# Preparing queries and keys tile by tile inside the q/k/v projection, with the rest of a convolution beside nine head groups

## What is computed

```python
h  = modulate(rms_norm(x), sh1, sc1);  proj = h @ w_in          # q 512 | k 128 | v 128 | glu 1024
q  = rope(rms_norm(q, q_norm_w));      k = rope(rms_norm(k, k_norm_w))   # per head of 64, 8 q heads, 2 k/v heads
k_ctx = rms_norm(...);  v_ctx = ...                              # context keys: normed, not rotated
s  = q @ [k_ctx, k in a window of +-128].T / 8;  p = softmax([sink, s])   # blocks of 128 queries
u  = ga * sigmoid(gb)
u  = depthwise_conv(u, 31 taps);  u = silu(layer_norm(u))        # 512 channels
x  = x + g1 * (concat(p @ v, u) @ w_out)                         # then the gated MLP
```

## Time and profile before

| what | value |
|---|---|
| median of 3 runs | 1344.73 us (1341.78 to 1345.15) |
| the profiled execution | 1338.05 us |
| its span, first to last instruction | 1336.2 us |
| mean granted TensorE clock | 0.964 |
| PE busy | 1227.3 us (92%) |
| PEld busy | 1014.5 us (76%) |
| DVE busy | 706.0 us (53%) |
| ACT busy | 429.0 us (32%) |
| POOL busy | 171.4 us (13%) |

### The profile page before, as it was taken

One profiled execution on the slowest core, in us unless ns is written; L12 is line 12 of the kernel. 1 busy time (PEld: TensorE's weight loads), 2 busy tenths in 40 slices (PEclk: granted clock), 3 DMA queues, 4 the chain that ended last, 5 costly groups with the idle time before them and its releaser, 6 DMA issues. The chain is left out here.

```text
span 1336.2 us, 15995 instructions
## 1 busy us (share of the span) xinstructions
PE 1227.3 (92%) x6181; PEld 1014.5 (76%) x6181; DVE 706.0 (53%) x950; ACT 429.0 (32%) x831; POOL 171.4 (13%) x146
## 2 busy tenths in 40 slices
PE   6899998259999989989999999999999969999997
PEld 1378887148998967878888888888888858887886
DVE  1489999866566553344434343434344344447445
ACT  4542144355665673443222222222222111111110
POOL 2100000359929100000000000000000000004001
PEclk9899999559999989999999999999999989999999
DMA  9222100015512123213111111111111041113112
GB/s 382 67 76 76 55 1 1 1 64 158 160 62 80 48 90 132 79 48 95 48 48 47 47 47 47 47 47 48 52 55 49 1 157 47 47 48 110 47 47 79
DMA packets 77988, 94.79 MB, mean 71 GB/s; under 512 B 5866, under 2 KB 59234, under 8 KB 76916
## 3 DMA queue, kind: packets, MB, share of 16 engines
q1 hardware_dynamic: 75796, 87.65, 20.2%
q10 hardware_dynamic: 1152, 4.19, 0.8%
q0 software_dynamic: 992, 2.29, 0.5%
HBM read 85.74 MB, written 8.39 MB: 70 GB/s over the span
## 5 line engine op out<-in xcount | busy, mean ns | idle before, releaser
L1281 PE MATMUL ps<-hx,uph 128*128 128x512 f32 x672 | 261.4, 389 | 0.0
L1282 PE MATMUL ps<-hx,uph 128*128 128x512 f32 x672 | 261.4, 389 | 0.0
L1285 PE MATMUL ps<-hx,upl 128*128 128x512 f32 x672 | 206.8, 389 | 0.0
L1083 DVE TENSOR_TENSOR upl<-up_raw,uph 128x1024 fp32r<-128x1024 f32 x44 | 53.8, 1226 | 263.9 <-ACT uph L1080 263.9
L1080 ACT ACTIVATE uph<-up_raw 128x1024 fp32r<-128x1024 f32 x44 | 46.6, 1060 | 339.4 <-PE ps L1285 328.5
L1414 PE MATMUL ps<-dnh,ah 128*128 128x512 f32 x352 | 138.0, 392 | 13.2 <-DVE al L1465 13.2
L1285 PEld LDWEIGHTS ps<-hx,upl 128*128 128x128 f32 x672 | 126.1, 188 | 26.2
L1282 PEld LDWEIGHTS ps<-hx,uph 128*128 128x128 f32 x672 | 126.2, 188 | 26.1
L1281 PEld LDWEIGHTS ps<-hx,uph 128*128 128x128 f32 x672 | 126.1, 188 | 26.2
L1415 PE MATMUL ps<-dnl,ah 128*128 128x512 f32 x352 | 137.5, 391 | 0.0
L1416 PE MATMUL ps<-dnh,al 128*128 128x512 f32 x352 | 137.4, 390 | 0.0
(11 more groups left out here) (241 smaller groups left out, 2169.8 us busy)
## 6 DMA issues: line engine op xcount, KB each, us to landing
up_raw<-in_w_up SPq DMA_DIRECT2D x44, 512.0 KB, 3.8
wm<-in_w_mod SPq DMA_DIRECT2D x32, 512.0 KB, 3.8
dn_raw<-in_w_down SPq DMA_DIRECT2D x44, 256.0 KB, 2.6
wm<-in_w_mod SPq DMA_DIRECT2D x8, 1024.0 KB, 20.2
xs<-in_x ACTq DMA_DIRECT2D x8, 512.0 KB, 14.5
gw_raw<-in_w_in SPq DMA_DIRECT2D x8, 512.0 KB, 4.0
wo_raw<-in_w_out SPq DMA_DIRECT2D x8, 512.0 KB, 3.4
xt<-in_x SPq DMA_DIRECT2D x8, 512.0 KB, 5.2
```

The lines of the kernel that those rows point to most:

```text
L1083: dve.tensor_tensor(out=upl[:, g], in0=up_raw[:, g], in1=f(uph[:, g]), op=ALU.subtract).then_inc(up_lo, 1)
L1281: pe.matmul(o, uph[:, g, k, :], hx[:, k, 0, c_], start=(k == 0), stop=False)
L1282: pe.matmul(o, uph[:, g, k, :], hx[:, k, 1, c_], start=False, stop=False)
L1285: last = pe.matmul(o, upl[:, g, k, :], hx[:, k, 0, c_], start=False, stop=(k == KT - 1))
```

## The change

Block 2 is gone and its work is in block 1, in the loop over the ten tiles.

- **PE** uses three pairs of banks in turn (`slot(m)`) instead of four, and banks 6 and 7 for the transposes. While it projects tile m it transposes the items of tile m-2 (`turn`), after the products of k = 2, 4 and 6: one item per context tile, three per latent tile. Six items are left behind the last tile.
- **ACT** squares the whole tile from PSUM in one instruction, copies out v alone, takes the square root, and writes the high parts `kst` and `qst` of the tile; `place` puts the transposes into `hx` (over the tokens already projected) and `kTc`. The placing of tile m-2 stands in front of the squares of tile m.
- **DVE** builds the tables first, then per tile rotates straight from PSUM (`rotated`), sums the squares with one reduction, adds the two parts of the rotation, norms the keys, and writes the low parts. Queries are not normed: their factor is the `scale` of the exponential and of line 992. POOL has no part in it. Per latent tile DVE runs 3 steps of the convolution.
- **Convolution**: of the 117 steps 24 stay beside the projection; 93 go into attention, 11 in each of groups 0 to 7 and 5 in group 8 (three after each of the first three `maxima`, two after the fourth).
- **Layer norm**: LN = 9, so the means are in groups 9 and 10, the variances in 11 and 12, the root in 12, and the reciprocals two each in groups 13 and 14. POOL scales `cacc` behind them.
- **Modulation vectors**: POOL still scales the 32 pieces, but adds them with a DMA of its own queue that accumulates into `sums`; the four vectors are summed in parallel, eight rounds of four.
- `wo_raw` is loaded once the convolution is done; the low parts of the outputs are stored in other places of `hx` (`out_rows`).

The diff, cut:

```diff
...
+        TAP_QKV = (0, 0) + (3,) * TT
+        TAP_GRP = 11
...
+            items = []
+            for m in range(NK):
+                items += [(m, "k")] if m < CT else [(m, "k"), (m, 0), (m, 1)]
...
+
+            def slot(m):
+                return 2 * (m % 3)
...
-                sp.wait_ge(gl_mm, NGL)
-                sp.dma_start(cs[:], rope.rearrange("w (t p) d -> p w t d", p=P)).then_inc(cs_in, 16)
+                sp.wait_ge(gw_lo, NGL)
+                sp.dma_start(tabs[:, 0:2], rope.rearrange("w (t p) d -> p w t d", p=P)).then_inc(cs_in, 16)
...
+                def turn(it):
+                    m, kind = items[it]
+                    if it == 0:
+                        pe.wait_ge(u_done, CTL)
+                    if it >= 2:
+                        pe.wait_ge(qkT_out, it - 1)
+                    if kind == "k":
+                        pe.wait_ge(k_lo, m + 1)
+                        src = [kst[:, m % 2, j // 2, j % 2, :] for j in range(4)]
+                    else:
...
+                        src = [qst[:, m % 2, 4 * kind + j].rearrange("p v d -> p (v d)") for j in range(4)]
+                    for j in range(4):
+                        last = pe.transpose(ps[:, 6 + it % 2, j * P:(j + 1) * P].bitcast(F32R), src[j], identr[:])
+                    last.then_inc(qkT, 1)
+
+                turned = 0
+                for m in range(NK):
+                    b = slot(m)
+                    if m < 3:
+                        pe.wait_ge(u_done, 3 if m < 2 else CTL)
+                    else:
+                        pe.wait_ge(v_out, m - 2)
+                        pe.wait_ge(k_mul, m - 2)
+                        if m - 3 >= CT:
+                            pe.wait_ge(q_mul, m - 2 - CT)
...
+                        if m >= 2 and k in (2, 4, 6) and turned < items_upto[m - 1]:
+                            turn(turned)
+                            turned += 1
                     last.then_inc(qkv_mm, 1)
+                while turned < len(items):
+                    turn(turned)
+                    turned += 1
...
+                def place(it):
+                    m, kind = items[it]
+                    act.wait_ge(qkT, it + 1)
...
+                    if m < CT:
...
+                    else:
+                        act.wait_ge(qkv_mm, m + 1)
+                        c_ = slice((m - CT) * P, (m - CT + 1) * P)
+                        dst = hx[:, 0:4, 1, c_] if kind == "k" else hx[:, 4 * kind:4 * kind + 4, 0, c_]
+                        src = src.rearrange("p (j k) -> p j k", j=4)
+                    act.activation(dst, src, ACT.Copy).then_inc(qkT_out, 1)
+
+                placed = 0
...
+                for m in range(NK):
+                    b = slot(m)
+                    while m >= 2 and placed < items_upto[m - 1]:
+                        place(placed)
+                        placed += 1
+                    h0 = 0 if m >= CT else NH
                     act.wait_ge(qkv_mm, m + 1)
+                    if m:
+                        act.wait_ge(ssq_done, m)
+                    act.activation(sqb[:, h0:, :], ps[:, b:b + 2, :].rearrange("p b n -> p (b n)")[:, h0 * HD:(NH + NG) * HD].rearrange("p (h d) -> p h d", d=HD),
+                                   ACT.Square).then_inc(sqb_done, 1)
+                    act.activation(vraw[:, m], ps[:, b + 1, NG * HD:KVC].rearrange("p (g d) -> p g d", g=NG), ACT.Copy).then_inc(v_out, 1)
+                    act.wait_ge(ssq_done, m + 1)
+                    act.activation(msq[:, m, h0:], msq[:, m, h0:], ACT.Sqrt, bias=eps_c).then_inc(root_done, 1)
+                    act.wait_ge(k_rot, m + 1)
+                    if m >= 2:
+                        act.wait_ge(qkT, items_upto[m - 2] + 1)
+                    for r in range(2):
+                        act.activation(kst[:, m % 2, :, 0, r * HD:(r + 1) * HD], ka[:, m % 2], ACT.Copy).then_inc(k_hi, 1)
                     if m >= CT:
...
-                        last = act.activation(sqj[:, m % 2, h, :], v, ACT.Square, accum_out=msq[:, m, h:h + 1])
...
+                        act.wait_ge(q_rot, m - CT + 1)
+                        if m - CT >= 2:
+                            act.wait_ge(qkT, items_upto[m - 1])
+                        act.activation(qst[:, m % 2, :, 0, :], h3(qa[:, m % 2, :]), ACT.Copy).then_inc(q_hi, 1)
...
-                taps(CTL * NCS)
...
+                def rotated(out_c, out_s, src, tab, t, heads, first_wait, signal):
...
+                        dve.tensor_tensor(out=b4[:, :, :, half, :], in0=a4[:, :, :, 1 - half, :],
+                                          in1=sn4[:, :, half, :].unsqueeze(1).to_broadcast([P, heads, 2, 16]), op=ALU.mult)
+                    dve.tensor_tensor(out=out_c.rearrange("p (h d) -> p h d", h=heads), in0=src.rearrange("p (h d) -> p h d", h=heads),
+                                      in1=tabs[:, tab, t:t + 1, :].to_broadcast([P, heads, HD]), op=ALU.mult).then_inc(signal, 1)
+
+                for m in range(NK):
+                    b, t, h0 = slot(m), m - CT, (0 if m >= CT else NH)
...
+                    dve.wait_ge(tab_done, 11)
+                    dve.wait_ge(v_out, m + 1)
+                    if m >= 2:
+                        dve.wait_ge(k_lo, m - 1)
+                    if m < CT:
+                        dve.tensor_tensor(out=kk, in0=ps[:, b + 1, 0:NG * HD].rearrange("p (g d) -> p g d", g=NG),
+                                          in1=qkw[:, 1:2, :].to_broadcast([P, NG, HD]), op=ALU.mult).then_inc(k_mul, 1)
                     else:
...
+                        rotated(flat(kk), flat(kr), ps[:, b + 1, 0:NG * HD], 0, t, NG, None, k_mul)
+                        if t >= 2:
+                            dve.wait_ge(q_lo, t - 1)
+                        rotated(qa[:, m % 2, :], qb[:, m % 2, :], ps[:, b, :], 2, t, NH, None, q_mul)
+                    dve.wait_ge(sqb_done, m + 1)
+                    dve.reduce_sum(msq[:, m, h0:], sqb[:, h0:, :], axis=AX.X).then_inc(ssq_done, 1)
+                    dve.wait_ge(k_mul, m + 1)
+                    if m >= CT:
+                        dve.tensor_tensor(out=kk, in0=kk, in1=kr, op=ALU.add).then_inc(k_mul2, 1)
+                        dve.wait_ge(q_mul, t + 1)
+                        dve.tensor_tensor(out=qa[:, m % 2, :], in0=qa[:, m % 2, :], in1=qb[:, m % 2, :], op=ALU.add).then_inc(q_rot, 1)
+                        dve.wait_ge(k_mul2, t + 1)
+                    dve.wait_ge(root_done, m + 1)
+                    dve.reciprocal(msq[:, m, h0:], msq[:, m, h0:]).then_inc(rr_done, 1)
+                    dve.wait_ge(rr_done, m + 1)
+                    dve.tensor_tensor(out=kk, in0=kk, in1=msq[:, m, NH:].unsqueeze(2).to_broadcast([P, NG, HD]), op=ALU.mult).then_inc(k_rot, 1)
+                    taps(dve, TAP_QKV[m])
+                    dve.wait_ge(k_hi, 2 * (m + 1))
+                    dve.wait_ge(k_rot, m + 1)
+                    for r in range(2):
+                        ins = dve.tensor_tensor(out=kst[:, m % 2, :, 1, r * HD:(r + 1) * HD], in0=kk, in1=f(kst[:, m % 2, :, 0, r * HD:(r + 1) * HD]),
...
+                    ins.then_inc(k_lo, 1)
+                    if m >= CT:
+                        dve.wait_ge(q_hi, t + 1)
+                        dve.tensor_tensor(out=qst[:, m % 2, :, 1, :], in0=h3(qa[:, m % 2, :]), in1=f(qst[:, m % 2, :, 0, :]),
+                                          op=ALU.subtract).then_inc(q_lo, 1)
...
-                for n in range(NMOD):
-                    if n >= NW:
-                        sp.wait_ge(mod_acc, n - NW + 1)
...
+                for k in range(KT):
+                    for a, sec in enumerate(SECTIONS):
...
+                sp.wait_ge(tap_done, CTL * NCS)
...
-                    pool.tensor_tensor(out=dst[:], in0=dst[:], in1=w, op=ALU.add).then_inc(mod_acc, 1)
+                for k in range(KT):
+                    for a in range(NW):
+                        pool.wait_ge(wm2_in[a], 16 * (k + 1))
+                        pool.tensor_scalar(wm2[:, a, :], wm2[:, a, :], nat[:, k, 0:1], 1.0, ALU.mult, ALU.mult).then_inc(mod_mul, 1)
...
+                        else:
+                            pool.wait_ge(mod_acc[a], 16 * k)
+                        pool.dma_start(sums[:, a, :], wm2[:, a, :], accum_op=ALU.add).then_inc(mod_acc[a], 16)
+                pool.wait_ge(rec5, 4)
+                for ct in range(CTL):
+                    pool.tensor_tensor(out=cacc[:, ct, :], in0=cacc[:, ct, :], in1=rstd[:], op=ALU.mult).then_inc(scaled, 1)
...
+                    pe.wait_ge(o_lo, n - 1)
+                    if n == LN:
+                        pe.wait_ge(tap_done, CTL * NCS)
+                    if n in (LN, LN + 1):
+                        mean_of(lambda ct: cacc[:, ct, :], n - LN, mean_mm)
+                    else:
+                        pe.wait_ge(sq5, CTL * (n - LN - 1))
+                        mean_of(lambda ct: sqc[ct], n - LN - 2, var_mm)
...
+                    elif n in (LN + 4, LN + 5):
```

(22 more changed lines are left out.)

410 lines of the change are left out of this document (138 added, 272 removed).

## The result

The changed kernel takes 1365.24 us (median of 4 runs, 1363.89 to 1373.56), the kernel before 1344.94 us (4 runs, 1341.78 to 1346.96): a ratio of 1.0166, 95% interval 1.0121 to 1.0211. It is slower, by 20 us: inside the range of the forecast and above the likeliest case's own, which ended at 1360. The profiled execution takes 1363.89 us (span 1362.1), where that of before takes 1338.05: +25.8 us from trace to trace, where the sum of the prediction said +3.7.

The account below looks back on a forecast made before the run. It took PE to wait while DVE works before attention, then to be busy for 180 of 187.5 us. Terms -37.5 - 1.3 + 12.5 + 16 + 14 = +3.7 us gave 1348 us against the median, range 1327 to 1372.

Parts of the forecast that it names:

- the likeliest case: Whole kernel: the forecast of 1348 us, chance 0.52, with its own range of 1338 to 1360 us.
- The start: Projection up to attention: attention starts at 252.1 instead of 289.6 us, -37.5 us, bounds -44 to -30.
- Group 0: First attention group: loses the mean, gets its convolution steps, 20.1 for 21.4 us, -1.3 us.
- Part 3: POOL's scaled pieces beside DVE's steps in attention: thirty pieces at 0.53 us stop steps, +16 us, bounds 0 to 36.
- Part 2: Attention groups 1 to 8: convolution steps on DVE are partly hidden, groups of 13.84 us, +12.5 us (10 to 15).
- the second rival: Groups 0 to 8: PE's clock falls in gaps, costing 15 to 30 us, 1368 us; chance 0.13.
- a clock of 1.00 in groups 1 to 8: Sign to look for in attention: PE's granted clock stays at 1.00 throughout groups 1 to 8.
- the bound of 0: Lower bound for POOL's pieces beside DVE's steps: no cost if steps aren't stopped; dropped by the skill's rule.
- Part 4: Attention groups 9 to 15: layer norm, reciprocals and POOL's scaling come in, POOL's additions go, +14 us (9 to 18).
- the third rival: Modulation sums: accumulating DMAs come one after the other, deciding from 7 us each; at 8 us, 1381 us; chance 0.06.
- the fourth rival: Projection tiles: preparation isn't hidden, PE waits in each, 11.5 us a tile, 16 us more, 1364 us; chance 0.06.
- the first, free steps: Attention: POOL's pieces don't stop DVE's convolution steps, 16 us less, 1332 us; chance 0.23.

Follow-up runs that it names:

- the run with the tables first: Against the changed kernel, the 13 DVE steps behind the last GLU column were issued in the second context tile: 1358.40 us.
- both pieces narrow: Against the changed kernel, the layer norm's four reciprocals and POOL's four scalings of the convolution were cut to 8 columns: 1354.87 us.
- the two last kernels: Changed kernel with rearranged steps (seven per latent tile, nine per group), earlier layer norm: 16 pieces held back, 1325.32 us; none held back, 1330.51 us.

## Why the forecast came out as it did

**The start** was right: -35.6 for -37.5 us. The wait was 6.5 us as predicted, latent tiles are 9.52 to 9.56 us apart from the second on (predicted 9.5), and the end took 10.4 us (243.57 to 253.97). The prediction misread by a slice (PE's hole is slices 6 to 8, counted from 0), its 20 items of 0.34 us make 6.8 and not 6.7, and its sum of a group makes 13.87 and not 13.84; none of it matters. The 1.9 us that were missing lie in two places. The first latent tile's products end 8.4 us later than before (177.50 for 169.12), where the wait and three transposed items make 7.5: the clock fell behind the wait, to 0.88 and 0.78 in the two windows of 10 us from 160 on. The prediction priced the wait alone, and the run with the tables first shows that wait and fall together were worth 9.1 us. The seven tiles from there to 243.57 take 66.1 us, where 59.4 plus 17 items of 0.34 make 65.2.

**Group 0** was wrong by 4.1 us: the step that failed took it as a group at PE's low clock with room for its steps, and put no piece beside it (the thirty pieces of Part 3 are all priced in groups 1 to 8). Four pieces are loaded by then and come in a row; without the scaling it takes 21.2 us (predicted 20.1), so the pieces are 3.0 of the 4.1.

**Groups 1 to 8** came out at +29.9 for +28.5, but by two errors that cancel. That the sum was hit is luck. Taken apart by the run without POOL's scaling: without it they take 116.5 us, +19.7 over before, where Part 2 said +12.5; the pieces add 10.2, where Part 3 said 16. Part 2 had the mechanism and the interval of the maxima right to 1%. It had the end of a group too short, because it took it from a group at full clock. That is the second rival in a small size: the clock did fall, to 0.81 on average from 290 to 390 us. It fell in seven stretches and came back each time. But as DVE sets the pace, it cost some 4 to 7 us (two single pairs of traces) and not the 15 to 30 of the rival. The statement "a clock of 1.00 in groups 1 to 8" was wrong, and groups 1 to 7 took 14.4 to 17.2 us, not 14 to 16. Part 3's mechanism is shown: steps take up to 2.44 us beside a scaling and 0.74 beside a DMA issue. This is what the Trainium skill says ("SBUF — State Buffer", "Who interferes with whom"), and the traces agree; the bound of 0 was rightly dropped. The size of Part 3 was too large: of the 27 scalings in groups 1 to 8 only 15 lengthened a step, by 10.6 us in all.

**Groups 9 to 15** is where the sum failed: +26.5 for +14. Two terms of Part 4 were too small. The means: 14.4 us of products, "less what idle time takes, +11". No idle time takes any. Groups 9 to 12 take 59.4 us where four clean groups take 42.6: +16.8, the products in full and 2.4 for the subtractions in two of them. A stretch in which PE is busy for 180 of 187 us could have said so. The last groups: reciprocals +4.6 and POOL's scaling +1.5 make 6.1, and groups 13 to 15 take 12.8 us more than before (36.3 for 23.5). Eleven of these go away with both pieces narrow. The term left out that a stall there can drop the clock for all that follows, as it did in this trace, and it priced the scaling by its end ("2 us before ACT asks for it") and not by the small sums that it stops. This is the very row that carried Part 3. ACT's root was moved as well and had no price; its cost stays open.

**The accumulating DMAs** take 8.0 us each to landing (the page's DMA issues), above the 5 us allowed and above the 7 from which the third rival decides. They cost nothing, since the four sums overlap: the last lands at 392.7 us. The rival's condition, one after the other, isn't met. The preparation was hidden, so the fourth rival falls too, and the first, free steps, as well.

**The number**: 1348 was 17 us under the median. The trace says 22, of which 12.5 are Part 4, 4.1 group 0, 1.9 the start, 1.6 the way to the output projection, 1.4 groups 1 to 8 and 0.7 the rest; 5 of them don't show in the medians, since the profiled execution lay 6.7 us under the median before and 1.4 under it after.

## What to carry to other kernels

Price a piece that is moved by what it stops at its new place, not by its length: here 11 us lay in small sums behind POOL's scaling, in reciprocals ahead of a maximum, and in the clock that fell behind them. Filling another engine's idle time works while that engine keeps some of it: seven steps in a projection tile are free, nine in an attention group cost less than eleven, and 13 ahead of a first tile cost 6.5 us of PE and 2.6 more by the clock that fell behind. Where two sources of loss can each trigger the same fall, take away both at once before either is called innocent, and take more than one trace before either is called guilty.

## What was not expected of the hardware

- The same instructions give different group times from trace to trace. Groups 1 to 8 take 126.6, 124.0, 131.0, 126.4, 128.4 and 123.9 us in six kernels that don't differ there, most of them with the clock low at other places. At the end the same holds for the two last kernels, whose traces agree up to group 13: one keeps 1.00, the other falls to 0.50, and that costs 7.5 us by group 15 (12.65 and 10.6 for 9.6 and 6.2 us). A difference of a few microseconds between two single traces of this kernel shows nothing by itself.
- A step and a scaling stop each other. A scaling that starts 0.1 us or more before the end of a step takes 1.39 to 2.15 us instead of 1.11, and the step beside or behind it up to 2.44 instead of 0.74. Two streams of back to back work can alternate, both slowed, as in group 0. It isn't always the first to come that goes first: the scaling of 303.41 us started inside one step, was passed by the next (0.74 us) and took 1.89, and only the third step was stopped (1.52).
- POOL's own part of an accumulating DMA of 512 KB is 0.87 us, and its loss to DVE is nil. The transfer takes 8.0 us to landing (median of 32), where a plain one took 2.6; but the first and the last, with fewer beside them, took 4.7 and 4.5, and the plain loads of the same size beside them took 6.3 where the kernel before had 3.8. So much of the 8.0 goes with how many were under way; no run took one alone.
